# RWKV gate projections made in the attention's rounds, triangular solver on two head pairs at once (three-layer sequence block, one core)

## What is computed

```python
xn = rms_norm(h, norm_w)
p = jnp.einsum('bsd,dn->bsn', xn, w_in)
p_tm = p[..., :SHIFT_COLS]                      # r, k, v, w_lo, a_lo
prev = jnp.pad(p_tm, ((0, 0), (1, 0), (0, 0)))[:, :-1]
p_tm = p_tm + (prev - p_tm) * mu_shift
y_rwkv = rwkv7_time_mix(p_tm, p[..., RWKV_GATE0:ATT0], ...)
y_att = mixed_dilated_attention(p[..., ATT0:ATT_GATE0], p[..., ATT_GATE0:])
h = h + jnp.einsum('bsm,md->bsd', jnp.concatenate([y_rwkv, y_att], -1), w_out)

# rwkv7_time_mix: per head, state 64 x 64, over 1024 steps
sa = jnp.einsum('bhvk,bhk->bhv', state, av_t)
state = state * w_t + sa[..., None] * bv_t + v_t[..., None] * k_t
y_t = jnp.einsum('bhvk,bhk->bhv', state, r_t)
# then group norm of y, plus the bonus, times silu(gate)
```

## Time and profile before

| what | value |
|---|---|
| runs shown | 3044.05, 3044.23, 3054.51 us; median 3044.23 |
| span of the profiled execution, first to last instruction | 3047.4 us (its own time is not listed apart; the span lies 3.2 above the median of the runs) |
| PE busy | 2825.7 us, 93% of the span |
| DVE, ACT, POOL busy | 1653.7, 1255.6, 361.1 us |
| mean granted clock of PE | 0.970 |
| attention rounds | from 1115 to about 1640 us |
| four units behind them | to 1687 us |
| preparation | 1687 to 2094 us, then 27.8 us to the recurrence |
| recurrence | 2121.8 to about 2460 us |

### The profile page before, as it was taken

One profiled execution on the slowest core, in us unless ns is written; L12 is line 12 of the kernel. 1 busy time (PEld: TensorE's weight loads), 2 busy tenths in 40 slices (PEclk: granted clock), 3 DMA queues, 4 the chain that ended last, 5 costly groups with the idle time before them and its releaser, 6 DMA issues. The chain is left out here.

```text
span 3047.4 us, 52649 instructions
## 1 busy us (share of the span) xinstructions
PE 2825.7 (93%) x21272; PEld 2206.7 (72%) x21272; DVE 1653.7 (54%) x3101; ACT 1255.6 (41%) x2310; POOL 361.1 (12%) x525
## 2 busy tenths in 40 slices
PE   8999999989998999999999999996887899989998
PEld 6666777766676777776777777775777777778776
DVE  3555665732357534556565555474466664652565
ACT  4344443221224445555554433443344334532234
POOL 0000000000000011111110056675340000000000
PEclk9988999999998999999999999998989999999999
DMA  3000111242224542323333335337534454421114
GB/s 116 28 14 22 42 42 36 73 158 70 69 80 131 162 145 65 78 72 78 79 81 86 112 134 165 125 124 279 169 98 145 150 199 140 152 81 49 35 62 152
DMA packets 187073, 312.39 MB, mean 103 GB/s; under 512 B 78144, under 2 KB 119376, under 8 KB 185296
## 3 DMA queue, kind: packets, MB, share of 16 engines
q1 hardware_dynamic: 186832, 309.04, 32.3%
HBM read 237.10 MB, written 71.89 MB: 101 GB/s over the span
## 5 line engine op out<-in xcount | busy, mean ns | idle before, releaser
L255 PE MATMUL ps<-xs,wparts 128*128 128x512 f32 x1664 | 698.6, 420 | 11.9 <-DVE xs L1515 9.3
L257 PE MATMUL ps<-xs,wparts 128*128 128x512 f32 x1664 | 655.0, 394 | 0.0
L256 PE MATMUL ps<-xs,wparts 128*128 128x512 f32 x1664 | 654.8, 393 | 0.0
L323 DVE TENSOR_TENSOR wparts<-wring,wparts 128x1024 fp32r<-128x1024 f32 x248 | 305.8, 1233 | 316.8 <-ACT wparts L315 292.9
L255 PEld LDWEIGHTS ps<-xs,wparts 128*128 128x128 f32 x1664 | 313.7, 189 | 130.9 <-issue 68.0
L315 ACT ACTIVATE wparts<-wring 128x1024 fp32r<-128x1024 f32 x248 | 263.0, 1061 | 275.3 <-PE ps L257 213.1
L257 PEld LDWEIGHTS ps<-xs,wparts 128*128 128x128 f32 x1664 | 313.5, 188 | 71.8
L256 PEld LDWEIGHTS ps<-xs,wparts 128*128 128x128 f32 x1664 | 314.4, 189 | 60.6 <-issue 4.8
L2269 POOL COPY perm<-qkg 128x1024 f32<-128x1024 f32 x32 | 63.1, 2008 | 1511.7 <-ACT qkg L359 1115.1
L2415 ACT ACTIVATE Pm<-Pm,ml 128x128 f32<-128x128 f32 (+1 forms) x384 | 168.0, 440 | 140.5 <-DVE ml L2483 140.4
L2483 DVE CUSTOM_DVE_ANT_0 Pm<-ps,mask 128x128 f32<-128x128 f32 (+1 forms) x384 | 110.9, 349 | 187.6 <-PE ps L2318 187.6
(11 more groups left out here) (408 smaller groups left out, 4868.3 us busy)
## 6 DMA issues: line engine op xcount, KB each, us to landing
wring<-in_wo SPq DMA_DIRECT2D x96, 512.0 KB, 3.5
ops<-rw SPq DMA_DIRECT2D x32, 640.0 KB, 6.1
wring<-in_w SPq DMA_DIRECT2D x39, 512.0 KB, 3.6
wring<-in_w2u SPq DMA_DIRECT2D x33, 512.0 KB, 4.4
wring<-in_wg SPq DMA_DIRECT2D x24, 512.0 KB, 3.6
wring<-in_w2v SPq DMA_DIRECT2D x24, 512.0 KB, 3.9
wring<-in_w2a SPq DMA_DIRECT2D x24, 512.0 KB, 6.6
MB<-wst SPq DMA_DIRECT2D x48, 256.0 KB, 5.0
```

The costliest lines, as they stand in the source:

```text
L255: nc.tensor.matmul(out, a, c, start=start, stop=False)
L256: nc.tensor.matmul(out, b, c, start=False, stop=False)
L257: return nc.tensor.matmul(out, a, d, start=False, stop=stop)
L323: K.nc.vector.tensor_tensor(W.part(i, 1), W.raw(i), W.part(i, 0).bitcast(F32), ALU.subtract).then_inc(*K.dve.done("w_lo", W.first + i))
```

## The change

The eight gate units of RWKV are made in the attention's rounds: four units a round (q, k, attention gate, RWKV gate), with one buffer `rg` that SP stores to DRAM at once. `host2` lays the weights out in the new order. In round 7 three units are spread over the steps instead of two. Behind the rounds stand r, k, v of pair 0 and r of pair 1. The preparation's groups get 3, 3, 3, 3, 3, 2, 2, 1 units; in the last one the last triangles and the first stage of the recurrence begin after 17 steps. The solver takes pairs 2j and 2j+1 on 128 partitions; its corners move with 8 DMAs each way in groups 2, 4 and 6 and once in the recurrence, and the last result is stored behind group 6 of the recurrence.

```diff
-OUT_W0, V_W0, ATT_W0, PREP_W0, LATE_W0 = 47, 71, 95, 119, 152
+OUT_W0, V_W0, ATT_W0, PREP_W0, LATE_W0 = 47, 71, 95, 127, 152
@@ prep_unit, prep_groups
-    return 1 + 4 * p + x
+    return 1 + 3 * p + x
+BEHIND, PASSES, LAST_AT = [(0, 0), (0, 1), (0, 2), (1, 0)], [3] * 5 + [2, 2, 1], 17
-    order, sizes = iter([(p, x) for p in range(1, NP) for x in range(4)]), [4] * 5 + [3, 3, 2]
-    return [[next(order) for _ in range(n)] for n in sizes]
+    order = iter([(p, x) for p in range(NP) for x in range(3)][len(BEHIND):])
+    return [[next(order) for _ in range(n)] for n in PASSES]
@@ prep_sp
+    first = [1 + len(BEHIND) + sum(PASSES[:p]) for p in range(NP)]
+    i = 6
     for p in range(NP):
-        for i in range(4 * p + 3 if p else 6, 4 * p + 7):
-            if i < 33:
-                yield from w_load(K, B.W, i)
-            if i in MB_AT:
-                yield from mb_store(K, A, B, MB_AT.index(i))
-            if i in SOLVE_AT:
-                yield from solve_move(K, A, B, SOLVE_AT.index(i))
-        if p:
-            yield from prep_store(K, A, B, p - 1)
-    yield from mb_store(K, A, B, NP - 2)
+        for at in (first[p] + 3, first[p] + 4, first[p] + 5):
+            while i <= min(at, 24):
+                yield from w_load(K, B.W, i)
+                i += 1
+            if at == first[p] + 3 and p:
+                yield from mb_store(K, A, B, p - 1)
+            if at == first[p] + 4 and p in (2, 4, 6):
+                yield from solve_move(K, A, B, p // 2 - 1)
+        if p < NP - 1:
+            yield from prep_store(K, A, B, p)
@@ solve_move (xt_store: the same two pairs)
-def solve_move(K, A, B, p):
+def solve_move(K, A, B, j):
-    K.sp.wait_ge(*(yield "mb_store", p, 3))
-    if p:
-        yield from xt_store(K, A, B, p - 1)
-        K.sp.wait_ge(*(yield "xt_store", p - 1))
-    for i, here, there in corners(A, B, p, 0):
+    for p in (2 * j, 2 * j + 1):
+        K.sp.wait_ge(*(yield "mb_store", p, 3))
+    if j:
+        yield from xt_store(K, A, B, j - 1)
+        K.sp.wait_ge(*(yield "xt_store", j - 1))
+    for p in (2 * j, 2 * j + 1):
+        for i, here, there in corners(A, B, p, 0):
@@ solve_pool (and the same for 128 partitions in every operation)
-        d = B.tmp[0:64, 0:s * n].rearrange("p (i t) -> p i t", t=n)
+        d = B.tmp[:, 0:s * n].rearrange("p (i t) -> p i t", t=n)
@@ prep_pe (prep_act, prep_dve alike)
-                                 *([triangles_pe(K, B, p), rwkv_first_pe(K, B.rw, B.RU)] if p == NP - 1 else [])),
+        yield from weave(in_turn(*[prep_unit_pe(K, B, *u) for u in units]),
+                         *([later(LAST_AT, in_turn(triangles_pe(K, B, p), rwkv_first_pe(K, B.rw, B.RU)))]
@@ att_sp
-        for i in range(3 * p + 4, 3 * p + 7):
+        for i in range(4 * p + 4, 4 * p + 8):
-            if p and i == 3 * p + 4:
+            if p and i == 4 * p + 4:
+                yield from rg_store(K, A, B, p - 1)
                 yield from weights_move(K, A, B, p - 1)
+def rg_store(K, A, B, p):
+    K.sp.wait_ge(*(yield "uev", ATT_W0 + att_unit(p, 3), 1))
+    K.nc.sync.dma_start(A["rw"][p][:, 6144:7168], B.rg).then_inc(*K.sp.done("rg_store", p, by=16))
@@ att_units_pe (att_units_act, att_units_dve alike)
         yield from att_unit_pe(K, B, p - 1, 2)
+        yield from att_unit_pe(K, B, p - 1, 3)
@@ att_order
-                         units(K, B, p + 1) if p < 7 else paced(fill(K, B), 1, 2))
+                         units(K, B, p + 1) if p < 7 else paced(fill(K, B), 2, 3))
@@ rwkv_sp
-    yield from solve_move(K, A, B.prep, NP - 2)
+    yield from solve_move(K, A, B.prep, NP // 2 - 1)
         if n == 6:
-            yield from solve_move(K, A, B.prep, NP - 1)
-        if n == 9:
-            yield from xt_store(K, A, B.prep, NP - 1)
-            K.sp.wait_ge(*(yield "xt_store", NP - 1))
+            yield from xt_store(K, A, B.prep, NP // 2 - 1)
+            K.sp.wait_ge(*(yield "xt_store", NP // 2 - 1))
```

More of the change, by code:

```diff
@@ L1629, in prep_layout @@
     B.cols = cols
[L1630 removed]
+    B.r, B.k, B.v, B.spare = [sb(n, [128, 2, 1024]) for n in ("r", "k", "vT", "spare")]
     B.Bc, B.Kc, B.bon = [sb(n, [128, 2, 1024]) for n in ("Bc", "Kc", "bon")]
@@ L1635, in prep_layout @@
     B.mbs = early[:, 1, 160:928].rearrange("p (c x) -> p c x", x=192)
-    last = [x[:, 0, 0:768].rearrange("p (c x) -> p c x", x=192) for x in (B.v, B.gate, B.Kc, B.bon)]
+    last = [x[:, 0, 0:768].rearrange("p (c x) -> p c x", x=192) for x in (B.v, B.spare, B.Kc, B.bon)]
     B.stage = lambda p, q: last[q] if p == NP - 1 else B.mbs
@@ L1686, in prep_early_sp @@
 def prep_early_sp(K, A, B):
-    for i in (1, 2):
+    for i in range(3):
         yield from w_load(K, B.W, i)
@@ L1743, in solve_move, with xt_store @@
-def solve_move(K, A, B, p):
-    K.sp.wait_ge(*(yield "mb_store", p, 3))
-    if p:
-        yield from xt_store(K, A, B, p - 1)
-        K.sp.wait_ge(*(yield "xt_store", p - 1))
-    for i, here, there in corners(A, B, p, 0):
-        K.nc.sync.dma_start(here, there).then_inc(
-            *K.sp.done("g_part", p, i, by=16, also=[("g_load", p)] if i == 3 else []))
-def solve_pool(K, B, p):
+def xt_store(K, A, B, j):
+    K.sp.wait_ge(*(yield "solved", j))
+    for p in (2 * j, 2 * j + 1):
+        for i, here, there in corners(A, B, p, 128):
+            K.nc.sync.dma_start(there, here).then_inc(
+                *K.sp.done("xt_part", p, i, by=16, also=[("xt_store", j)] if p % 2 and i == 3 else []))
@@ L1759, in solve_pool @@
+def solve_move(K, A, B, j):
[4 more added lines that the diff above has]
+        K.sp.wait_ge(*(yield "xt_store", j - 1))
+    for p in (2 * j, 2 * j + 1):
+        for i, here, there in corners(A, B, p, 0):
+            K.nc.sync.dma_start(here, there).then_inc(
+                *K.sp.done("g_part", p, i, by=16, also=[("g_load", j)] if p % 2 and i == 3 else []))
+def solve_pool(K, B, j):
     nc, pool = K.nc, K.pool
-    G = B.G[0:64, :].rearrange("p (i t) -> p i t", t=32)
@@ L1932, in prep_act @@
     for p, units in enumerate(prep_groups()):
-        yield from weave(in_turn(*[prep_unit_act(K, B, *u) for u in units],
-                                 *([rwkv_first_act(K, B.rw)] if p == NP - 1 else [])), prep_small_act(K, B, p))
+        yield from weave(in_turn(*[prep_unit_act(K, B, *u) for u in units]),
+                         *([later(LAST_AT + 12, rwkv_first_act(K, B.rw))] if p == NP - 1 else []), prep_small_act(K, B, p))
     barrier(K, act, 3)
@@ L2089, in prep_pool @@
     nc.gpsimd.memset(B.mbs[:, :, 128:192], 0.0).then_inc(*pool.done("mb_zero"))
-    for p in range(NP):
-        yield from solve_pool(K, B, p)
+    for j in range(NP // 2):
+        yield from solve_pool(K, B, j)
 def att_layout(K, A, st, xs, W, b1):
```

107 lines of the change are left out of this document (52 added, 55 removed).

## The result

The change takes 3037.27 us (median of 12 runs, 3033.34 to 3051.26). The kernel before took 3045.55 us in the same comparison (12 runs, 3040.64 to 3056.01). The ratio is 0.9974, 95% interval 0.9963 to 0.9985: 8 us faster, within the 0.5% that was forecast as "same", 0.3 us from the forecast's number. The profiled execution took 3039.89 us, its span is 3038.6. The sum of the forecast was right; several of its terms were not.

The account below looks back on a forecast made before the run. PE was taken to bound preparation and attention, bytes counted from X the preparation's end. Terms -17.6 + 10.9 + 8.1 + 3.4 - 8.7 - 1.4 - 1.9 = -7.2 us, from 3044.2 to 3037 us; range 3023 to 3055.

Parts of the forecast that it names:

- X: End of the preparation: the moment SP may issue the recurrence's first operands, at 2088.18 before; claimed to set the recurrence's start.
- Attention, -17.6: Rounds 0 to 6: the fourth unit covers four of PE's five small waits, 2.52 us a round; 0.94 stays bare.
- The fourth rival: Attention: PE's waits only wander, so the 17.6 us gain goes; +10.4, 3055 us; chance 0.10.
- Round 7, 0: Attention's round 7: a weight load wanted four steps earlier and three covering units instead of two cancel; bounds -6 and +6.
- One unit more, +10.9: Ahead of group 7 of the preparation: one unit of 33 left when it begins instead of two, costing 10.9 us.
- groups 5 and 6, +8.1: Preparation groups with two units: PE, with 33.4 us of work, waits 5.3 and 2.8 us for DVE's line; bounds 0 and 18.0.
- clock +3.4: Ends of groups 5 and 6: two new PE waits may each lower the clock, 1.7 us lost each; bounds 0 and 6.9.
- Group 7 to X, -8.7: From group 7's first triangles to X: 27.8 us instead of 36.5, as SP no longer waits for the solver; bounds 26 and 36.5.
- End, -1.4: From X to the recurrence: the same bytes less one gate store of 512 KB, 1.4 us at 363 GB/s.
- Recurrence, -1.9: Recurrence: two solves become one; a group beside busy POOL took 29.4 us, its twin with POOL idle 27.5.
- one rival about it, on its partitions: Solver on 128 partitions: if its step cost doubled, operands come late; +7, 3051 us; chance 0.05.
- The forecast's larger figure of 0.61 for DVE: DVE meeting POOL: by an exclusive lock each meeting could cost DVE 0.61 us instead of 0.25; halving solver instructions worth some 4.

## Why the prediction was right, and where not

Its number was right because errors of its terms cancelled; that it came within 0.3 us is luck. Against the forecast the attention gave 3.6 us more, round 7 with the units behind it 1.9 more and the end 0.4 more; the short groups took 1.3 more, group 7 to X 4.2 more, and the last stretch 3.2 more. So behind the first scores the trace has -4.4 us for the forecast's -7.2; the other 4.4 of the spans' difference lie ahead of them, where nothing was changed.

- *Attention, -17.6*: measured 465.9 + 76.3 - 521.0 = 21.2 us gained. The prediction had left the last wait of each round; it went too, and no run tests why. The fourth rival, that the waits only wander, did not happen.
- *Round 7, 0*: the term left out too much. Of PE's waits of 2.72 and 2.42 us there only 1.19 stayed, and the low clock behind the first went, a bound that the prediction had priced at -6. It had nothing on the place behind: the fourth unit there changed from a gate to a projection with a shift. Together -1.9, made of gains of some 8 and the new 5.8 at small 0.
- *One unit more, +10.9, and groups 5 and 6, +8.1, clock +3.4*: the mechanism was right and the sizes nearly so. The groups took 40.0 and 38.2 us (forecast 38.7 and 36.2), PE waited 6.6 and 3.1 us (5.3 and 2.8), and the clock fell behind both (0.58 and 0.50), at small 0 (0.67), and in group 7. Stage by stage +12.8 for a forecast of +11.5.
- *Group 7 to X, -8.7*: the failed step; measured -4.5. The prediction took the 36.5 us for SP's delay alone and a group 5 without it, 29.4, as what would be left. X before was the end of PE's last unit; the solver acted on it through DVE and `D`, by the wait of 2.5 us and 1.7 lost in the 3.4 us at half the clock, 4.2 of the 4.4 us that the pairing alone brought. With that gone 32.1 remain with the units, and with the change 32.0, by another cause: the mask's place behind `D` and `AR`. The run with the early mask shows it, 25.3. Beside that the forecast's 27.8 had sizes wrong: it counted 0.9 us for DVE beside a busy POOL, and the run without the solver's work has 2.5; and it took off 2.5 for the store's wait, which was indeed short in the change (0.74 us), but DVE then waited 3.2 us for PE's triangles instead.
- *End, -1.4*: 1.8 measured. That X sets the recurrence's start is borne out by all fourteen traces, in which X moves by 61 us and this distance by less than 2.
- *Recurrence, -1.9*: wrong. The group that had a solve beside it took 29.4 us and its twin without 27.5. Now POOL is idle in both, and they take 29.6 and 29.2. What the rows of before had differed in as well is the clock, 0.83 against 0.88; in the change it is 0.83 and 0.82. These are the two stretches before, then the two of the change:

```profile
2221.92:2251.31 29.39, 22.74 (x596) 20.90 (x592) 19.91 (x44) 12.37 (x30) 26.33 (x40) 0.83 0.25 79
2311.58:2339.05 27.47, 21.92 (x595) 20.57 (x592) 18.18 (x43) 11.94 (x29) 0.00 (x0) 0.88 0.24 79
```

```profile
2210.32:2239.87 29.55, 23.64 (x594) 22.27 (x592) 18.18 (x43) 11.98 (x29) 0.00 (x0) 0.83 0.23 73
2302.84:2332.04 29.20, 23.66 (x595) 22.28 (x592) 18.17 (x44) 11.99 (x29) 0.00 (x0) 0.82 0.21 75
```

  At the same clock of 0.83 the group took 29.4 us beside a busy POOL and 29.6 beside an idle one. So the difference of the clock had been taken for POOL's price. The whole stretch of one program varied by 7 us.
- *The pairing*: the prediction gave it 1.9 us and part of the 8.7, and had only one rival about it, on its partitions. It had no rival in which the solver is too slow for shorter groups. The page had a sign of it, in the chain of waits of the kernel before, by engine and by line:

```profile
PE 28%; DVE 8%; ACT 2%; DMA 2%; POOL 1%; issue 1%; SPq 1%; DVEq 0%; ACTq 0%
PE ps L255 7%; PE ps L257 6%; PE ps L256 6%; PE ps L2601 6%; DMA mx<-early 1%; DVE wparts L323 1%; POOL step L1768 1%; POOL solve L1772 1%; PE ps L2610 1%; ACT wparts L315 1%; DMA wring<-in_wo 0%; PE ps L3317 0%; PE ps L3303 0%; DVE mk__54 L2946 0%; SPq L1707 0%
```

and in that of the change the solver is gone:

```profile
PE 29%; DVE 8%; ACT 2%; issue 1%; DMA 1%; SPq 0%; DVEq 0%; ACTq 0%
PE ps L255 7%; PE ps L2618 6%; PE ps L257 6%; PE ps L256 6%; DVE wparts L323 1%; PE ps L2627 1%; ACT wparts L315 1%; DVE mk__55 L2961 1%; DMA wring<-in_wo 0%; PE ps L3332 0%; PE ps L3318 0%; PE ps L1827 0%; PE ps L1835 0%; ACT dg L2867 0%; DVE y L3668 0%
```

In the chain of the kernel before the solver's two lines have 0.7% of the span each, together some 43 us, the length of about one solve. A solver that takes some 53 us a pair and groups that go from 55 to 44 us should have been set beside each other first.

What stays open: why the last wait of a round went, why group 6 took longer without the solver's work, and why the stretch behind the recurrence's start takes 918 to 935 us in kernels whose edits hardly touch it. That last spread is larger than the whole gain of the change, so one profile of each kernel could not have told the gain.

## What to carry to other kernels

A moved piece of work is paid for where it comes from: PE gained 23 us net up to the preparation, and gave 19 of them back: 12.8 in groups too short for DVE's line, 6.4 at an event that another engine sets (group 7 to X lost a unit of 10.9 us and became only 4.5 shorter). Ask of each event on the path which of its waits ends last, now and after the change; twice here it was not the one that the profile had shown before. And where stages get shorter, compare the new period with every engine that has a fixed time for each of them, however idle it looks: POOL was busy for 12% of the span and would have cost some 45 us.

## What the runs showed of the hardware

Where POOL and DVE meet, the one that begins second waits for the other. The solver's operations of this size take 0.59 to 0.66 us by themselves, as the first row does; the next two stood beside two operations of DVE:

```profile
1887.63 0.59 POOL L1772 TENSOR_TENSOR step<-solve 128x228 f32<-128x228 f32 x1
1888.31 2.49 POOL L1776 TENSOR_TENSOR solve<-solve,step 128x228 f32<-128x228 f32 x1
1890.87 1.47 POOL L1772 TENSOR_TENSOR step<-solve 128x234 f32<-128x234 f32 x1
```

```profile
1887.93 2.44 DVE L1989 TENSOR_TENSOR_SCAN early<-early 128x1024 f32<-128x1024 f32 x1 [3.93 <-ACT early L1901]
1890.48 1.40 DVE L323 TENSOR_TENSOR wparts<-wring,wparts 128x1024 fp32r<-128x1024 f32 x1
```

Each of POOL's last two began while DVE's was running, and ended 0.43 and 0.46 us behind the end of DVE's (1890.37 and 1891.88). Each of DVE's began while an operation of POOL was running, and it paid as well: the second took 1.40 us where it takes 1.23 alone, and ended 1.08 us behind POOL's end at 1890.80. That figure is a rule here. In the fourteen traces, from 1687 to 2180 us, 248 operations of DVE with two inputs of 128x1024 in SBUF began with more than 0.17 us left of a solver's operation; every one ended 1.08 to 1.09 us behind the end of that operation, so it paid what was left of it less 0.14 us, up to 0.42 us. With less than 0.15 us left (42 of them), or when POOL began after it (26), it took its 1.22 to 1.23 us and paid nothing. Nor did the 393 operations of DVE that read one of their 128x512 inputs from PSUM: 0.69 us, whatever was left of POOL's. So POOL pays more only because DVE's operations are longer. The Trainium skill, page "SBUF — State Buffer", section "SBUF: two separate sides", says that the one that starts first gets the pair for the whole instruction and that the other fully blocks; the traces agree, but for the first 0.14 us of the second. The forecast's larger figure of 0.61 for DVE falls, since a meeting costs what is left of an operation and not the whole; its 0.25 was one such remainder. The same skill's page "GPSIMD Engine Reference", section "Extended-addressing connectivity", has each core on its own 16 partitions, and 634 against 635 ns for twice the partitions agrees.
